# Sums of squares as products of rounded parts, and two filler tiles moved to the front stage of a decoder layer

## The reference

```python
h = rmsnorm(x, norm_mix);  z = h @ w_in          # ten 256-wide branch inputs, four 1024-wide gates
qa, ka = rmsnorm per head of 64 (q_norm, k_norm)  # branch A: stick-breaking attention
o_b = rmsnorm per head (hgrn2(...)) * silu(gb)    # branch B, chunkwise recurrence
x = x + sum_n(sigmoid(gate_n) * (branch_n @ w_branch[n])) @ w_out
x = x + conv_ffn(rmsnorm(x, norm_ffn))
x = x + sigmoid(rmsnorm(x, norm_ple) @ w_ple_gate) * (p @ w_ple)
# rmsnorm(x) = x * rsqrt(mean(x * x) + eps) * g, in float32
```

## Time and profile before

| | |
|---|---|
| runs | 1757.38, 1755.03, 1757.04 us; median 1757.04 |
| profiled execution | 1755.68 us, its span 1753.9 us |
| busy, share of the span | PE 99%, DVE 63%, ACT 42%, POOL 44% |
| front pairs | 106 to 292 us |
| head norms, attention | 569 to 608 us, 608 to 729 us |
| mix stage | 729 to 850 us |
| last gate | 1652 to 1752 us |

### The profile page before, as it was taken

The page is one execution under the profiler, slowest core; times in us unless marked ns, Lnnn a source line. Parts: engine busy times, 40 slices in busy tenths (PEclk is TensorE's granted clock), DMA queues, the critical chain, the costliest instruction groups (busy, mean ns, idle before and its releaser), DMA issues.

```text
span 1753.9 us, 30899 instructions
## 1 busy us (share of the span) xinstructions
PE 1730.0 (99%) x12865; PEld 1678.6 (96%) x12865; DVE 1113.4 (63%) x1255; ACT 730.9 (42%) x1034; POOL 776.1 (44%) x531
## 2 busy tenths in 40 slices
PE   8999999999999999999999999999999999999998
PEld 8999999998999877899999999999999999999998
DVE  6931115826674267657744877888888887675744
ACT  6433334443421456612235554444444442333621
POOL 1666773431222212212123476677776636667021
PEclk9999999999999999999999999999999999999999
DMA  6543226132221532557523223232222375334032
GB/s 229 76 121 119 100 75 215 37 106 75 69 81 68 191 115 68 165 180 250 206 76 143 90 81 110 99 118 102 98 99 98 117 285 208 117 118 147 26 126 96
DMA packets 84798, 214.80 MB, mean 122 GB/s; under 512 B 14866, under 2 KB 32050, under 8 KB 83506
## 3 DMA queue, kind: packets, MB, share of 16 engines
q1 hardware_dynamic: 73714, 189.48, 31.5%
q0 software_dynamic: 4032, 14.68, 2.7%
q10 hardware_dynamic: 6912, 8.65, 1.4%
HBM read 149.48 MB, written 63.40 MB: 121 GB/s over the span
## 4 chain that ended last, share of the span: by engine, by line
PE 92%; DVE 3%; ACT 2%; DMA 1%; issue 1%; POOL 1%; SPq 0%; ACTq 0%; DVEq 0%; POOLq 0%
PE ps L1637 24%; PE ps L1087 21%; PE ps L1074 11%; PE ps L1685 10%; PE ps L1217 10%; PE ps L1669 3%; PE ps L1305 2%; PE ps L1172 1%; PE ps L1390 1%; PE ps L1061 1%; PE ps L1114 1%; DMA masks<-in_wb 1%; PE ps L1554 1%; PE ps L1424 1%; PE ps L1411 1%
## 5 line engine op out<-in xcount | busy, mean ns | idle before, releaser
L3323 POOL TENSOR_TENSOR Wl<-BIG,Wh 128x512 fp32r<-128x512 f32 x110 | 142.9, 1308 | 117.9 <-ACT Wh L2181 117.8
L3180 POOL CAST Uh<-BIG 128x1024 fp32r<-128x1024 f32 x27 | 36.0, 1333 | 289.3 <-PE ps L1074 199.1
L2974 DVE SCALAR_TENSOR_TENSOR ps<-BIG,fpar,ps 128x1023 f32<-128x1023 f32 x84 | 108.0, 1285 | 36.0 <-ACT ps L2272 35.1
L1074 PE MATMUL ps<-Hh,Uh 128*128 128x352 f32 x384 | 128.3, 334 | 0.8 <-ACT BIG L1922 0.8
L1074 PE MATMUL ps<-Hh,Ul 128*128 128x352 f32 x384 | 123.6, 322 | 0.0
L1074 PE MATMUL ps<-Hl,Uh 128*128 128x352 f32 x384 | 123.3, 321 | 0.0
L2535 DVE TENSOR_TENSOR BIG<-BIG,ps 128x528 f32<-128x528 f32 x45 | 31.6, 704 | 144.2 <-PE ps L1217 143.9
L3275 POOL TENSOR_TENSOR Ul<-BIG,Uh 128x1024 fp32r<-128x1024 f32 x15 | 36.1, 2412 | 164.7 <-ACT Uh L2141 164.7
L1637 PE MATMUL ps<-Hl,Wh 128*128 128x264 f32 x528 | 107.1, 284 | 0.0
L2963 DVE TENSOR_TENSOR BIG<-BIG,ps 128x528 f32<-128x528 f32 x110 | 77.4, 703 | 42.9 <-PE ps L1637 37.1
L1685 PE MATMUL ps<-Sl,Vh 128*128 128x264 f32 x504 | 101.9, 283 | 0.0
(11 more groups left out here) (467 smaller groups left out, 5557.7 us busy)
## 6 DMA issues: line engine op xcount, KB each, us to landing
BIG<-in_wu SPq DMA_DIRECT2D x44, 512.0 KB, 4.5
hidden<-BIG SPq DMA_DIRECT2D x22, 528.0 KB, 2.8
late_gates<-BIG SPq DMA_DIRECT2D x18, 528.0 KB, 3.0
BIG<-sums SPq DMA_DIRECT2D x12, 792.0 KB, 4.7
BIG<-in_wgl SPq DMA_DIRECT2D x9, 1024.0 KB, 6.1
BIG<-in_wd SPq DMA_DIRECT2D x6, 1536.0 KB, 10.2
H<-late_gates SPq DMA_DIRECT2D x17, 528.0 KB, 3.6
gates<-BIG ACTq DMA_DIRECT2D x48, 176.0 KB, 2.0
```

Of the source, the lines that this page charges most:

```text
L1074: ins = nc.tensor.matmul(psb(fill_bank(p)), w[:, u % 2, k], x[:, k, part * PART:part * PART + PART], start=(k == 0 and w is Uh and x is Hh ...
L2974: link(v.scalar_tensor_tensor(y[:, back:SEQ], x[:, 0:SEQ - back], w, y[:, back:SEQ], ALU.mult, ALU.add), v.scalar_tensor_tensor(ys[:, :, b ...
L3323: nc.gpsimd.tensor_tensor(Wl[:, b], src, Wh[:, b].bitcast(F32), ALU.subtract).then_inc(S("w_lo"), 1)
```

## The change

Two things are changed.

First, seven sums of squares (four head norms, the one ahead of the feed-forward without its last row, and two of the last norm) become products of rounded parts by a rounded matrix: the constant matrices are rounded in place (their entries are powers of two), the row is split into high and low, and each span takes two rounded matmuls (`two_parts`). In head norms DVE squares, ACT squares into the high part and DVE subtracts. The first of the two residual sums is split by DVE after the seventh row. The last row's own sum stays in full precision. The last norm's sums are split by DVE, and `final_sums` moves from the end of tile 0 to behind the first nine matmuls of tile 1.

Second, of the gates of branches 2 and 3, two tiles are no longer fillers but the pair number 8 of now ten pairs. 14 filler tiles are left, 42 parts: `start1` has 2 instead of 3, `norms` 6 instead of 8, `steps` 10 instead of 13 (no parts at steps 18, 22 and 28). All later parts get other numbers, so banks and the ends of tiles shift: the parts of `out1` are 24 and 25 (they were 25 and 26), those of `states1` 14 and 15 (15 and 16). The last two parts of `norms` use banks 6 and 7. The two gates get their sigmoid in the front.

```diff
 LATE = 8 - EARLY
+EARLY_OF = (3, 3, 2, 2)
...
 UNITS = 4 * EARLY
-FILLS = QKS + UNITS
+FILL_UNITS = [(i, n) for i in range(4) for n in sorted(TURN_OF[0:EARLY_OF[i]])]
+FILLS = QKS + len(FILL_UNITS)
...
 COVER = 2
-PAIRS = (4 * LATE - COVER) // 2
+MOVED, MOVED_PAIR = ((2, TURN_OF[2]), (3, TURN_OF[2])), 8
+PAIRS = (4 * LATE + len(MOVED) - COVER) // 2
...
 WLO, WHI = ULO + 2 * UP, COVER + 2 * UP - 3
-PLACES = (("states0", 2), ("levels0", 8), ("out0", 2), ("start1", 3), ("states1", 2), ("levels1", 8), ("out1", 2),
-          ("norms", 8), ("steps", 13))
-TWO_BANKS = 34
+PLACES = (("states0", 2), ("levels0", 8), ("out0", 2), ("start1", 2), ("states1", 2), ("levels1", 8), ("out1", 2),
+          ("norms", 6), ("steps", 10))
...
 SHORT = 8
-FILL_STEPS = {s: j for j, s in enumerate((0, 2, 6, 8, 10, 14, 16, 18, 20, 22, 24, 28, 30))}
+FILL_STEPS = {s: j for j, s in enumerate((0, 2, 6, 8, 10, 14, 16, 20, 24, 30))}
...
-    odd = p % 2 ^ (p in parts("start1"))
-    return 6 if p == TWO_BANKS else 2 if p < TWO_BANKS and odd else 5
+    odd = p % 2 ^ (p in parts("start1")) ^ (p in parts("norms"))
+    last = parts("norms")[4:]
+    return 6 + (p - last[0]) % 2 if p in last else 2 if p < last[0] and odd else 5
...
             def pair_weights(c, sem):
-                src = a["wgl"].rearrange("i v p k m -> (i v) p k m")[COVER + 2 * c:COVER + 2 * c + 2]
+                first = COVER + 2 * (c - (c > MOVED_PAIR))
+                src = (a["wge"].rearrange("(i n) p k m -> n i p k m", n=EARLY)[MOVED[0][1], MOVED[0][0]:MOVED[1][0] + 1]
+                       if c == MOVED_PAIR else a["wgl"].rearrange("i v p k m -> (i v) p k m")[first:first + 2])
...
+            def two_parts(out, w, hi, lo, last=True):
+                for g, (t0, n) in enumerate(SPANS):
+                    for x in (hi, lo):
+                        ins = nc.tensor.matmul(psb(3 * out + g), w, x[:, t0:t0 + n], start=x is hi,
+                                               stop=last and x is lo)
+                return ins
...
-            for p in parts("norms")[:-1]:
-                if p == parts("norms")[1]:
+            late = parts("norms")
+            for p in late[:4]:
+                if p == late[1]:
...
             for j in range(4):
-                if j == 0:
-                    pe.wait_ge(S("gate_out"), parts("norms")[-3] + 1)
-                    pe.wait_ge(S("b_over"), 2)
-                elif j == 1:
-                    pe.wait_ge(S("gate_out"), parts("norms")[-2] + 1)
-                if j == 2:
-                    fill(parts("norms")[-1], (0,))
-                pe.wait_ge(S("a_sq"), j + 1)
-                if j >= 2:
+                pe.wait_ge(*upto("a_lo", j + 1))
+                if j < 2:
+                    pe.wait_ge(S("gate_out"), late[2 + j] + 1)
+                else:
                     pe.wait_ge(S("a_ln"), j - 1)
-                whole(1 - j % 2, cc("headmean"), nsq[j % 2])\
-                    .then_inc(S("a_ms"), 1)
-            fill(parts("norms")[-1], (1,))
+                two_parts(j % 2, headmean_r, nhi[j % 2], nlo[j % 2]).then_inc(S("a_ms"), 1)
+                if j == 1:
+                    fill(late[4])
+                elif j >= 2:
+                    fill(late[5], (j - 2,))
...
             pe.wait_ge(S("r_added"), KD - 1)
-            pe.wait_ge(S("r_ss"), KD - 1)
-            whole(0, cc("mean"), nSS, last=False).then_inc(S("norm_sum"), 1)
+            pe.wait_ge(S("r_ss"), KD)
+            two_parts(0, mean_r, nSSh, nSSl, last=False).then_inc(S("norm_sum"), 1)
...
                 pe.wait_ge(S("r_sq"), KD)
-                whole(0, cc("mean"), nSQ7, first=False).then_inc(S("norm_sum"), 1)
+                whole(0, mean_r.bitcast(F32), nSQ7, first=False).then_inc(S("norm_sum"), 1)
...
             def final_sums():
-                pe.wait_ge(S("d_added"), ENDED)
-                pe.wait_ge(S("r_ss"), 2 * KD - 2)
-                pe.wait_ge(S("r_sq"), 2 * KD)
+                pe.wait_ge(S("r_ss"), 2 * KD + 1)
...
                         pe.wait_ge(S("n1_ln"), 5)
-                    nc.tensor.matmul(pst[g % 2][:, 0:n], cc("mean"), dSS[:, t0:t0 + n], start=True, stop=False)
-                    nc.tensor.matmul(pst[g % 2][:, 0:n], cc("mean"), dSQ[:, t0:t0 + n], start=False, stop=True)\
-                        .then_inc(S("norm_sum"), 1)
+                    for x in (dSSh, dSSl, dSQh, dSQl):
+                        ins = nc.tensor.matmul(pst[g % 2][:, 0:n], mean_r, x[:, t0:t0 + n], start=x is dSSh,
+                                               stop=x is dSQl)
+                    ins.then_inc(S("norm_sum"), 1)
...
                     dense3(1 - q, (Uh[:, q], Ul[:, q]), normed_x, KD, ("n2_h", 1) if c == 0 else None,
-                           (KD - 1, final_sums) if c == 0 else None).then_inc(S("p_gate"), 1)
+                           (0, final_sums) if c == 1 else None).then_inc(S("p_gate"), 1)
...
                     act.wait_ge(S("a_normed"), j - 1)
-                nc.scalar.activation(spans(nrs[j % 2]), slab(1 - j % 2), ACT.Ln, bias=epsc).then_inc(S("a_ln"), 1)
+                nc.scalar.activation(spans(nrs[j % 2]), slab(j % 2), ACT.Ln, bias=epsc).then_inc(S("a_ln"), 1)
...
-            order = (KA, KA + 1, QA, QA + 1)
-            for p in parts("norms")[:-2]:
-                gate_out(p)
-            act.wait_ge(S("b_over"), 2)
-            for j in range(4):
+            def square_high(j):
...
                 act.wait_ge(S(f"rows_in{j // 2}"), 32)
-                nc.scalar.activation(nsq[j % 2], Z[:, order[j], :], ACT.Square).then_inc(S("a_sq"), 1)
-                if j == 1:
-                    gate_out(parts("norms")[-2])
-                if j >= 1:
-                    a_rs(j - 1)
+                nc.scalar.activation(nhi[j % 2], Z[:, NORM_ORDER[j], :], ACT.Square).then_inc(S("a_sq"), 1)
+            late = parts("norms")
+            for p in late[:3]:
+                gate_out(p)
+            act.wait_ge(S("b_over"), 2)
+            square_high(0)
+            square_high(1)
+            gate_out(late[3])
+            a_rs(0)
+            square_high(2)
+            a_rs(1)
+            gate_out(late[4])
+            square_high(3)
+            a_rs(2)
             a_rs(3)
-            gate_out(parts("norms")[-1])
+            gate_out(late[5])
...
                     row_high(s)
-                if s < 5 or s % 8 < EARLY:
-                    if s % 8 < EARLY:
+                if s < 5 or early(s):
+                    if early(s):
...
                         act.wait_ge(S("m_added"), s - 1)
-                    nc.scalar.activation(spans(gate_row(s)), spans(gate_row(s)) if s % 8 < EARLY else slab(1),
+                    nc.scalar.activation(spans(gate_row(s)), spans(gate_row(s)) if early(s) else slab(1),
...
             dve.sem_inc(S("a_set"), 1)
-            rs = nrs
-            for j in range(4):
+            def square(j):
+                if j >= 2:
+                    dve.wait_ge(S("a_ms"), j - 1)
+                dve.wait_ge(S(f"rows_in{j // 2}"), 32)
+                row = Z[:, NORM_ORDER[j], :]
+                link(v.tensor_tensor(nsq[j % 2], row, row, ALU.mult))
+            def square_low(j):
+                dve.wait_ge(S("a_sq"), j + 1)
+                v.tensor_tensor(nlo[j % 2], nsq[j % 2], nhi[j % 2].bitcast(F32), ALU.subtract).then_inc(on("a_lo"), 1)
+            def head_normed(j):
                 dve.wait_ge(S("a_rs"), j + 1)
-                if j < 2:
-                    link(v.scalar_tensor_tensor(Z[:, KA + j, :], Z[:, KA + j, :], pc("k_norm"), rs[j % 2], ALU.mult,
-                                                ALU.mult))
-                else:
-                    link(v.scalar_tensor_tensor(Z[:, QA + j - 2, :], Z[:, QA + j - 2, :], pc("q_norm"), rs[j % 2],
-                                                ALU.mult, ALU.mult))
+                row = Z[:, NORM_ORDER[j], :]
+                link(v.scalar_tensor_tensor(row, row, pc("k_norm" if j < 2 else "q_norm"), nrs[j % 2], ALU.mult, ALU.mult))
...
+            link(v.tensor_copy(mean_r, cc("mean")), v.tensor_copy(headmean_r, cc("headmean")))
+            for j in range(2):
+                square(j)
+                square_low(j)
+            for j in range(2):
+                square(j + 2)
+                head_normed(j)
+                square_low(j + 2)
+            head_normed(2)
+            head_normed(3)
...
                         v.tensor_tensor(nSS, nSS, nSQ, ALU.add).then_inc(S("r_ss"), 1)
+                if c == KD - 2:
+                    dve.wait_ge(S("r_ss"), KD - 1)
+                    link(v.tensor_copy(nSSh, nSS))
+                    v.tensor_tensor(nSSl, nSS, nSSh.bitcast(F32), ALU.subtract).then_inc(S("r_ss"), 1)
...
                 square_sum(d)
+            dve.wait_ge(S("r_ss"), 2 * KD - 1)
+            dve.wait_ge(S("r_sq"), 2 * KD)
+            link(v.tensor_copy(dSSh, dSS), v.tensor_copy(dSQh, dSQ))
```

(34 more changed lines are left out.)

13 lines of the change are left out of this document (7 added, 6 removed).

## The result

The changed kernel takes 1765.44 us (median of five runs, 1764.60 to 1766.07) against 1757.04: ratio 1.0051 [1.0041, 1.0061], **8.4 us slower**. The direction was forecast (+4.5), the size was not: by the spans of the two profiled executions the change costs 9.0 where the sum said 5.0.

A forecast was written before the change was run, and what follows sets the result against it. TensorE, busy 99% of the span, was taken as the bound. Terms summed to +5.0 us on 1755.68, giving 1760.7; 1.4 for the median, less half a us: 1761.5. Likeliest range 1759 to 1765; 8 in 10, 1752.5 to 1766.

The forecast's parts named there:

- the paragraph on the clock: Whole kernel: TensorE keeps its full clock of 2.4 GHz, no wait being over 2.4 us; nothing added to the sum.
- Attention's ring: Attention: scores, ScalarE's sigmoids and copy pace TensorE; removed parts at steps 18, 22, 28 give 1.7, 0.9, 2.0: -4.6 us.
- half clock: Rival in attention: TensorE work around the thinned steps doubles in time, adding 11 us, total 1772; chance 0.03.
- Front: Front stage: one more pair, 168 products of 264 columns that nothing hides, +20.6 us.
- final sums: Last norm: rounded products 1.9 plus 0.3 for a bank instead of 3.3, after VectorE's casts and subtractions; net -0.8 us.
- levels1: Second round's levels: GpSimd's displaced split delays VectorE's factor passes and TensorE waits, +2.5 us (bounds 0 to 3.2).
- out1: Second round's output stage: last filler in another bank, so the norm's product need not wait for ScalarE's copy, -0.7 us.
- Head norms: Six parts and shorter sums, but VectorE's chain and GpSimd's split make sums late: 31.9 for 39.0, -7.1 us.
- Mix: Mix stage: two gates need no sigmoid there, so GpSimd's pass holds VectorE one us less; -0.9 us (0 to -1.4).
- POOL finding gaps: Rival: GpSimd's passes hold nobody up; levels1 +0, head norms -10, total 1756.1; chance 0.24.
- no ring: Rival in attention: TensorE gets all 11.6 us of the removed parts back, total 1754.5; chance 0.16.
- rounded sums not cheaper: Rival: rounded sums cost as much as full ones, three us more in head norms, one at the end: 1766; chance 0.04.

The follow-up runs named there:

- experiment 2: Changed kernel with ScalarE's first two squares of head norms moved ahead of its copy of the third filler part; 1762.29 us, ratio 1.0035 to the kernel before.
- experiment 1: Changed kernel plus 42 products nobody reads, in TensorE's waits in head norms and at attention steps 18, 22 and 23; 1760.95 us, ratio 1.0029 to the kernel before.
- 3: Changed kernel with GpSimd's splits of two tiles, ahead of the second round's levels and in head norms, held back by two filler parts; 1761.42 us, ratio 1.0028.
- 10: Kernel of 8 with the two filler parts of the second round's output stage in the other two banks; 1750.51 us, ratio 0.9972 to the kernel before.
- 7: Changed kernel with the four sums of head norms in full precision again, without their low parts; 1764.45 us, ratio 1.0047 to the kernel before.
- 6: Changed kernel with SyncE's issue of the first w_out tile moved ahead of its wait for the last gate store; 1764.75 us, ratio 1.0045 to the kernel before.
- 9: Changed kernel with attention steps 24, 28 and 30 without filler parts in place of 18, 22 and 28; 1762.82 us, ratio 1.0036 to the kernel before.
- 8: Kernel before with rounded sums alone, no moved pair, head norms' squares and low parts earlier, GpSimd's split there held back; 1750.32 us, ratio 0.9971.
- 11: Changed kernel with experiment 1, experiment 2, 3 and 6 together, head norms in the order of 8; 1757.09 us, ratio 1.0007 to the kernel before.
- 12: Kernel of 11 without 6, the first w_out load back behind the wait for gate stores; 1758.65 us, ratio 1.0012 to the kernel before.

## Why the prediction was wrong in size

**What failed** is the paragraph on the clock: "My sum keeps the full clock: no wait in it is over 2.4 us, the start's was 6.5." This put the clock at nothing, and two things were wrong in it. Its own ring has PE stand longer: of the 3.85 us of the part at step 22 only 0.9 come off, so 2.95 are waits (measured 3.2, in two pieces). And the wait at the start was no measure: the granted clock fell behind waits of 2.5, of 2.0 plus 1.2, and of 2.2 us in head norms, though not in every trace (experiment 2). The rows of before could not show it, as fillers left no idle stretch over 1.3 us in them but the start's. In attention it cost 3.1 of the 3.4 us that the term missed (experiment 1). The Trainium skill (TensorE: Matmul & The Clock Gate, "What's actually happening"), cited there, says that an idle engine runs at half its clock until it has worked again. The traces agree on the two levels (0.51 behind the waits, 1.00 once they were filled). The rival *half clock* was priced at 11 us for a persistent fall and given 0.03; what came in the changed kernel were three short falls.

**Point by point.**
- *Front, start1, final sums*: as worked out, within 0.4.
- *levels1*: the mechanism was right and shown by taking it away (3), 2.05 for 2.5: the pass stretched across the split was seen where it was foreseen.
- *out1*: right, 0.9 for 0.7; confirmed by 10 in the trace only.
- *Head norms*: the stage's -7.1 came out as -7.6, in part by luck. Sum 1 stood 2.2 us for its low part, for 2.4 foreseen; 2 took the wait away whole by ScalarE's order, and the split held that low part for 0.7 of it (1.97 us for 1.26). Sum 2, 1.4 late in the steps, did not stand at all, because the products ahead of it ran at the lower clock; with the clock kept up (1) it stood the 1.4. VectorE's chain, which the steps had right, ends the stage either way. The "gain of 12.1" was what PE's products alone would give; 7 shows that in this order the four rounded sums were a loss of 1.2.
- *Attention's ring*: right. The scores stand 5.84 apart (693.71 - 687.87) for 5.95 foreseen, and 7.22 (718.85 - 711.63) for 7.4. With the clock kept up the term is 4.4 for 4.6.
- *To the mix stage*: no term stood for it; 0.6, which lies within the 0.2 to 1.0 of the other traces (6).
- *Mix*: "-0.9" happened at the wait foreseen (0.80 us there for 1.61 before), but the second w_out tile's wait grew by as much, from 0.80 to 1.68.
- *Feed-forward*: 0.5 us, which three of the twelve other traces show too and nine do not; not explained.
- *Rivals*: POOL finding gaps is out (3), no ring is out (9, and the spacings), rounded sums not cheaper is out (final sums).

## What to carry to other kernels

Work that fills a wait is worth its time only where nothing else is late just behind it: ask of each filler taken away what the engine will stand for next, and how long. Where that stand is like the 2 to 3 us seen here, count with a stretch behind it at the lower clock as a case with a chance of its own, or put unread products into it. And compare a cheaper operation by all its passes: a sum 0.8 us shorter on PE that adds two VectorE passes can be a loss where VectorE's chain ends the stage, until the passes are put in a better order (7, 8).

## What the runs showed of the hardware that was not expected

- The granted clock was at 0.51 behind waits of 2.2 to 3.3 us (1.9 to 3.0 of idle in the records), but 1.00 behind a wait of 2.21 us of idle in one trace of five; and it fell once in three traces behind idle stretches of at most 0.8 us. 42 products that nobody reads won some 4 us.
- A VectorE pass of 0.69 us with two SBUF inputs took 2.84 when a GpSimd subtraction of 2.39 had begun 0.1 us ahead of it, and a pass of 1.25 took 3.43.
- The same mix stage took 4 to 5 us more in the traces of the two mended kernels (11, 12) than in others with the same code there, 3.0 and 1.8 of them at the lower clock behind a wait of 2.7 us of idle.
